# Paired projection in a hybrid GLA / Gated DeltaNet layer: x operands in two sets, fill slots and copies in another order

## The chip, the cores and the metric

One core of one Trainium2 chip, everything in float32. The metric is the device time of one execution in microseconds (us), the median of several runs. Engines are named as in the profile: PE (TensorE), PEld (its weight load), DVE (VectorE), ACT (ScalarE), POOL (GpSimd), SP (SyncE, which here only issues DMAs).

## The reference

One layer: RMSNorm, one input projection of 3608 columns, two head groups (GLA and Gated DeltaNet), an output projection with a residual, RMSNorm, and a gated MLP with a short convolution, for a prompt of 2048 tokens and eight sample sequences of four.

```python
hn = rmsnorm(x, norm1_g[l])
proj = hn @ w_in[l]                       # 1024 -> 3608
q_a, k_a, v_a, gate_a, low_a, qkv_b, z_b, beta_b, dec_b = jnp.split(proj, IN_IDX, axis=-1)
...
log_a = log_sigmoid(low_a @ gla_w_a2 + gla_b_a) / GLA_TAU
o_a, h_a = gla_chunked(q, k, v, log_a, st_gla[l])
o_a = rmsnorm(o_a, gla_norm_g) * silu(gate_a)
qkv, conv_new = causal_dwconv(qkv_b, st_conv[l], gdn_conv_w[l])   # width 4
qd, kd, vd = jnp.split(silu(qkv), ...)                            # q, k l2-normed
o_b, h_b = gdn_chunked(qd, kd, vd, g, beta, st_gdn[l])            # triangular solve in it
o_b = rmsnorm(o_b, gdn_norm_g) * silu(z_b)
x = x + concat(o_a, o_b) @ w_out[l]
x = x + (silu(a_f) * b_f) @ w_down[l]     # a_f, b_f: convolved up-projection of rmsnorm(x)
```

## The kernel before

The program has two stages. `mixers()` does all but the MLP, to 1765 us of the profiled execution; `mlp()` does the rest and is the same in both kernels. The prompt is cut into 16 tiles of 128 tokens (t = 0 to 15), and the sample is one more tile.

**One tile.** In each tile PE transposes the tile's `proj` (L1036 to L1059), multiplies for the decay sums (L1065 to L1077), and computes the GLA scores over seven levels (L1099 to L1104), which DVE copies with `turn_levels` (L1828). The short convolution is 48 DVE operations in four taps (`conv_tap`, L1846 and L1848) with a tanh on ACT (L1557) and the silu's end on DVE (L1959). The silu of both gates is two DVE operations (L1938). PE then transposes q, k and v (L1114, L1126, L1120), computes the GLA output (L1135, L1137), and inverts a triangular matrix in seven doubling levels a = 0 to 6. In each level POOL makes `ltm` (`ex<-dtt,level`, L842), PE multiplies (L1207, L1202), and DVE copies between. The state update and the outputs end the tile (L1281 to L1315); `gate_out` (DVE L2068) scales the outputs, and PE turns them (`turn_mixed`, L1196) for the next tile's output projection (L1002). `turn_y` (PE L1027) transposes the previous tile's normed sum.

**The input projection in the gaps.** Tiles 0 to 13 also compute the projection of the next pair of tiles by a Strassen-like scheme: 14 products per tile, each in two parts of two matmuls of 128x451. `fill(a, b)` in the PE program issues what stands in the slots a to b-1. `PRODUCT_SLOTS` gives the slot of each of the 28 parts, `OUT_SLOTS` that of each of 8 parts of the output projection. Three things feed the products:

- *Weight sums.* Ten chunks per tile, loaded by SP (`ring_chunk`, L526 from `sums_d`, L523 from the weights) into four places. A chunk's load waits until the products have used its place. The sums are made by DVE at the start (`first_sums`, `second_sums`, L1730) and stored by SP (L509).
- *x operands.* DVE scales two 128x1024 column blocks (`scaled_columns`, L1717) at the end of an even tile; POOL makes seven 128x512 operands from them in eight operations (L861 to L871) between an odd tile and the next.
- *Results.* ACT copies (`keep`, L1444) or DVE adds (`make_c11`, `make_c12`, `make_c22`, L1751) each product into one of eight `stage` buffers, SP stores them (L541), and `load_proj` (L553 to L560) reads the next tile's `proj`. `load_proj` waits for the gates' silu, the last reader of the old `proj`. The ring chunks n+4 and on (n = 10t) stand behind it in SP's order; the first product to read chunk n+4 is q = 6, parts 12 and 13.

The row scales of the columns take a way through memory: `store_scale` (L499) and `load_scales` (L504), both on SP.

**What sets the order.** Each engine's program is written out by hand in Python, with semaphores between them; no scheduler moves anything. A wait holds all that stands behind it on its engine. The two tables:

```python
OUT_SLOTS = {0: 0, 1: 1, 2: 2, 3: 3, 4: 4, 6: 5, 8: 6, 10: 7}
PRODUCT_SLOTS = {slot: p for p, slot in enumerate([5, 7, 9, 11, 12, 14, 15, 16, 17, 18, 20, 21, 22, 24] + list(range(25, 39)))}
```

## Time and profile before

| | |
|---|---|
| median of 3 runs | 3429.21 us (3424.32 to 3431.96) |
| profiled execution, its own time | 3427.54 us |
| its span, first to last instruction | 3425.8 us |
| mean granted TensorE clock, as a share of full speed | 0.957 |
| busy share of the span | PE 93%, DVE 62%, ACT 24%, POOL 19% |
| first projection and weight sums | 0 to 135.6 us |
| tiles 0 to 13, with the paired projection | 135.6 to 1532.0 us |
| tiles 14, 15 and the sample | 1532.0 to 1765.3 us |
| MLP | 1765.3 to 3425.8 us |

A tile is some 100 us: tile 4 begins (first L1077) at 523.71, tile 5 at 620.91 and tile 6 at 721.25 us. PE carries most of the work, so the time is what PE does, at the clock it is granted, and what it waits for. PEclk of 1.00 is 2.4 GHz and 0.50 is 1.2 GHz, the two levels that the profile shows. A row of a timeline may stand for several instructions ("x8"), whose first start and whole length it gives.

### The profile page before, as it was taken

Reading aid. Unit: us, or ns where it says so; the run is one execution under the profiler, and the core shown is the slowest. Engines: PE = TensorE matmul, PEld = TensorE weight load, DVE = VectorE, ACT = ScalarE, POOL = GpSimd, SP = SyncE. Lnnn points to the kernel's source line nnn. Section 1 sums busy time; section 2 is a strip of 40 time slices with the busy share of each in tenths; the row PEclk is TensorE's granted clock in tenths of the full one; section 3 lists DMA queues with packets and bytes.
Section 4 is the critical chain, followed back from the end, with each engine's and each line's share of the span. In section 5 each row is a group of like instructions: output and inputs, shape, how many; then the busy total and the mean of one; then the engine's idle time right before and its main releaser. Section 6 shows DMA issues by size and latency. Waiting matters only on the chain. (4 is left out here: it accounts for less than half of the span.)

```text
span 3425.8 us, 56382 instructions
## 1 busy us (share of the span) xinstructions
PE 3186.7 (93%) x22129; PEld 2094.5 (61%) x22129; DVE 2132.8 (62%) x4778; ACT 825.7 (24%) x1743; POOL 640.9 (19%) x985
## 2 busy tenths in 40 slices
PE   9699999999899998977679999999998999999999
PEld 4355555555555555544457777777767677767765
DVE  2666656666665666547555666656685665666668
ACT  1222222323132232212332121121222212212223
POOL 1212111120212112011223111112125121121110
PEclk9899999999999999988689999999999999999999
DMA  8655656556465656653561111111124111111112
GB/s 301 253 172 171 220 182 202 183 204 202 157 212 175 200 183 195 195 183 97 164 191 34 53 37 49 37 38 49 50 82 149 50 37 37 38 49 50 37 37 74
DMA packets 278999, 430.77 MB, mean 126 GB/s; under 512 B 20604, under 2 KB 203812, under 8 KB 277587
## 3 DMA queue, kind: packets, MB, share of 16 engines
q1 hardware_dynamic: 278739, 427.20, 38.8%
q8 instruction: 176, 2.88, 0.3%
q14 instruction: 84, 0.69, 0.1%
HBM read 361.44 MB, written 65.70 MB: 125 GB/s over the span
## 5 line engine op out<-in xcount | busy, mean ns | idle before, releaser
L970 PE MATMUL mixer_bank<-arena 128*128 128x451 f32 x1568 | 677.3, 562 | 0.4 <-issue 0.4
L2496 PE MATMUL mlp_bank<-arena,ws 128*128 128x256 f32 (+1 forms) x2816 | 648.3, 383 | 9.6 <-ACT raw L2686 9.6
L2496 PEld LDWEIGHTS mlp_bank<-arena,ws 128*128 128x128 f32 x2816 | 536.0, 190 | 92.8 <-ACT raw L2686 10.4
L2570 PE MATMUL mlp_bank<-arena 128*128 128x512 f32 x1120 | 493.9, 592 | 0.0
L970 PEld LDWEIGHTS mixer_bank<-arena 128*128 128x128 f32 x1568 | 281.6, 194 | 210.4 <-issue 204.3
L2971 DVE TENSOR_TENSOR acc<-acc,mlp_bank 128x512 f32<-128x512 f32 x560 | 370.3, 685 | 55.5 <-PE mlp_bank L2570 54.7
L2570 PEld LDWEIGHTS mlp_bank<-arena 128*128 128x128 f32 x1120 | 213.1, 190 | 234.5 <-issue 205.8
L842 POOL TENSOR_TENSOR ex<-dtt,level 128x512 f32<-128x512 f32 (+1 forms) x114 | 143.9, 1262 | 984.6 <-DVE dtt L1992 674.6
L2938 DVE SCALAR_TENSOR_TENSOR mcv<-raw,cf,mcv 128x512 f32<-128x512 f32 (+2 forms) x352 | 264.5, 767 | 59.4 <-ACT mcv L2659 50.6
L1002 PE MATMUL mixer_bank<-wo,th 128*128 128x512 f32 x512 | 266.3, 651 | 18.0 <-DMA wo<-in_w_out_dram 17.1
L2496 PE MATMUL mlp_bank<-arena 128*128 128x256 f32 (+1 forms) x1056 | 249.1, 386 | 5.3 <-PEq L3084 4.4
L2496 PE MATMUL mlp_bank<-arena,wu 128*128 128x256 f32 (+1 forms) x1056 | 246.0, 383 | 0.9 <-ACT raw L2688 0.9
L2496 PEld LDWEIGHTS mlp_bank<-arena 128*128 128x128 f32 x1056 | 201.1, 191 | 57.0 <-issue 26.4
L2496 PEld LDWEIGHTS mlp_bank<-arena,wu 128*128 128x128 f32 x1056 | 200.5, 190 | 49.2 <-issue 19.1
L2882 DVE TENSOR_TENSOR raw<-raw,mlp_bank 128x256 f32<-128x256 f32 (+1 forms) x88 | 37.5, 426 | 276.7 <-PE mlp_bank L2496 276.7
L1444 ACT COPY arena<-mixer_bank 128x451 f32<-128x451 f32 x112 | 59.7, 533 | 592.4 <-PE mixer_bank L970 592.3
L1002 PEld LDWEIGHTS mixer_bank<-wo,th 128*128 128x128 f32 x512 | 100.6, 208 | 142.8 <-issue 96.5
L2876 DVE TENSOR_TENSOR raw<-raw,mlp_bank 128x256 f32<-128x256 f32 (+1 forms) x88 | 37.5, 426 | 191.3 <-ACT raw L2688 191.3
L1848 DVE SCALAR_TENSOR_TENSOR cv<-cx,cw,cv 128x128 f32<-128x128 f32 x576 | 154.7, 344 | 0.0
L2659 ACT ACTIVATE mcv<-raw,cf 128x512 f32<-128x512 f32 (+2 forms) x176 | 126.8, 722 | 107.5 <-DVE raw L2882 85.6
L2642 ACT COPY raw<-mlp_bank 128x256 f32<-128x256 f32 (+1 forms) x88 | 33.1, 377 | 493.2 <-PE mlp_bank L2496 493.2
L2801 POOL COPY raws<-raw 128x32 f32<-128x32 f32 x44 | 7.8, 212 | 557.1 <-DVE raw L2882 557.1
(392 smaller groups left out, 4027.5 us busy)
## 6 DMA issues: line engine op xcount, KB each, us to landing
arena<-sums_d SPq DMA_DIRECT2D x112, 902.0 KB, 6.8
wo<-in_w_out_dram SPq DMA_DIRECT2D x260, 256.0 KB, 3.0
arena<-in_w_in_dram SPq DMA_DIRECT2D x44, 902.0 KB, 5.1
arena<-in_w_up_dram SPq DMA_DIRECT2D x44, 512.0 KB, 4.9
wu<-in_w_up_dram SPq DMA_DIRECT2D x44, 512.0 KB, 4.9
arena<-in_w_down_dram SPq DMA_DIRECT2D x40, 512.0 KB, 4.2
proj_d<-arena SPq DMA_DIRECT2D x84, 225.5 KB, 5.6
sums_d<-arena SPq DMA_DIRECT2D x16, 902.0 KB, 4.7
```

The costliest lines, as they stand in the source:

```text
L842: gp.tensor_tensor(ltm[0:N, :, 0:N], lt[0:N, :, 0:N], level[0:N, l, 0:N].unsqueeze(1).to_broadcast([N, H, N]), ALU.mult)\
L970: x = pe.matmul(out[:, 0:GW], xops[:, left, k, :], right[:, k, :], start=first and k == 0, stop=k == HK_IN - 1, skip_group_check=not first)
L1002: pe.matmul(bank[e if t == TILES else 3 + e][0:N, :], mixt[k // H][:, k % H, 0:N], wo[i % 4][:, :], start=(k == 0), stop=(k == KT - 1)).th ...
L1444: act.copy(stage[4 * (q // 7) + block], bank[source][:, 0:GW]).then_inc(s_kept, 1)
L1848: x = dve.scalar_tensor_tensor(out=dst, in0=src, scalar=cw[:, c, tap:tap + 1], in1=dst, op0=ALU.mult, op1=ALU.add)
L2496: x = pe.matmul(out[:, 0:N], left[:, k, :], xb[:, slot, k, g * N:(g + 1) * N], start=first and k == 0, stop=k == HK - 1, skip_group_check= ...
L2570: pe.matmul(bank[4 + o % 4][:, :], left, right, start=True, stop=True).then_inc(s_down_done, 1)
L2659: act.activation(cv[e][:, 0:n], raw[p][e][:, c0:c0 + n], ACT.Identity, scale=cf[p][:, e, 0:1])\
L2876: dve.tensor_tensor(v, v, q_bank[:, 0:N], ALU.add).then_inc(s_q1_added, 1)
L2882: dve.tensor_tensor(v, v, q_bank[:, 0:N], ALU.add).then_inc(s_q2_added, 1)
L2938: x = dve.scalar_tensor_tensor(out=dst, in0=src, scalar=w, in1=dst, op0=ALU.mult, op1=ALU.add)
L2971: dve.tensor_tensor(v, v, bank[4 + o % 4][:, :], ALU.add).then_inc(s_y_added, 1)
```

## The change

1. The order of the first projection, of its weight loads and of the sums: all four `first_sums` come ahead of all four `second_sums`, the stores follow that order, and the 16 `wo` chunks are loaded behind them.
2. The x operands lie in two sets (`x_set`, `sum_set`), used in turn. POOL makes a pair's operands in six operations, two of them 128x1024, in steps behind levels a = 2 to 6 of the odd tile before. DVE's two column scalings stand in levels a = 4 and 5 of the even tile.
3. `stage` has four buffers and not eight; two `keep`s wait for stores.
4. The two tables of slots; `turn_y(0)` and `turn_y(1)` go from level a = 1 to a = 2 and 3, the DVE work behind them likewise.
5. On ACT, `qsq` and `ked` stand ahead of the sum's norm and the next x tile's norm.
6. The gates' silu stands behind the GLA levels and `make_c22(t, 0)`. The convolution's end is split: tanh of q and k, then of v, and three silus with a semaphore step each; `turn_levels(3, 6)` goes ahead of `make_c11(t, 0)`.
7. The scaling of `hgdn` stands ahead of a reduce at the tile's end; `store_scale`, `load_scales` and `store_hs` move in SP's order.

```diff
-FIRST = [(g, tile) for g in (4, 0, 5, 1, 6, 7) for tile in range(2)] + [(2, 1), (3, 1), (2, 0), (3, 0)]
+FIRST = [(g, tile) for g in (4, 5, 6, 7, 0, 1) for tile in range(2)] + [(2, 1), (3, 1), (2, 0), (3, 0)]
-OUT_SLOTS = {0: 0, 1: 1, 2: 2, 3: 3, 4: 4, 6: 5, 8: 6, 10: 7}
-PRODUCT_SLOTS = {slot: p for p, slot in enumerate([5, 7, 9, 11, 12, 14, 15, 16, 17, 18, 20, 21, 22, 24] + list(range(25, 39)))}
+OUT_SLOTS = {0: 0, 1: 1, 2: 2, 3: 3, 4: 4, 6: 5, 9: 6, 11: 7}
+PRODUCT_SLOTS = {slot: p for p, slot in enumerate([5, 7, 10, 12] + list(range(14, 26)) + [27] + list(range(29, 40)))}
...
+                if t < TILES - 4:
+                    store_scale(t + 4)
                 ring_chunk(n + 8)
                 if even:
                     store_block(t, 0, C12)
                 store_block(t, 0, C21)
+                if t < TILES - 4 and not even:
+                    load_scales(t + 3)
...
+                    if prepares and a >= 2:
+                        x_operands((t + 1) // 2, (a - 2,))
+            def x_operands(p, steps):
+                source = (xc, hnt) if p == 0 else x_of(p)
+                if 0 in steps:
+                    gp.wait_ge(s_rsb_loaded, 16 * (p + 1))
+                    gp.wait_ge(s_xg_made, p + 1)
...
+                for e in range(2):
+                    if e in steps:
+                        gp.tensor_tensor(x_of(p)[e][:, :, :], source[e][:, :, :],
+                                         rsb[:, e, :].unsqueeze(1).to_broadcast([C, KT, C]), ALU.mult)\
+                            .then_inc(s_xops_made, 1)
+                if 2 in steps:
+                    gp.tensor_tensor(s1, a21, a22, ALU.add).then_inc(s_xops_made, 1)
+                if 3 in steps:
+                    gp.tensor_tensor(s2, s1, a11, ALU.subtract).then_inc(s_xops_made, 1)
+                    gp.tensor_tensor(a21, a11, a21, ALU.subtract).then_inc(s_xops_made, 1)
+                if 4 in steps:
+                    gp.tensor_tensor(s4, a12, s2, ALU.subtract).then_inc(s_xops_made, 1)
...
+                act.wait_ge(s_q_turned, n)
+                act.activation(qsq[0:N, :, :], heads(3)[0:N, :, :], ACT.Square).then_inc(s_q_squared, 1)
+                act.wait_ge(s_kl_turned, n)
+                act.copy(ked[0:N, :], bank[6][0:N, 256:512]).then_inc(s_ked_out, 1)
...
                 if out and not sample:
                     y_square(t, C)
-                    act.wait_ge(s_y_normed, 3 * t - 2)
+                    y_log(t, C)
+                    y_root(t, C)
                 front(0)
+                front(1)
+                front(2)
...
                 if hosts:
                     make_c22(t, 0)
+                for g, c0 in enumerate((O_GA, O_Z)):
+                    dve.wait_ge(s_gates_tanh, 3 * t + g + 1)
+                    dve.scalar_tensor_tensor(out=gate[...], in0=gate[...], scalar=1.0,
+                                             in1=proj[0:N, c0:c0 + H * DV], op0=ALU.add, op1=ALU.mult)\
+                        .then_inc(s_gates_silu, 1)
...
+            first_sums(2, 4)
+            first_sums(3, 6)
             dve.wait_ge(s_xc_loaded, 32)
...
-            second_sums(1, 6)
-            first_sums(2, 8)
-            first_sums(3, 10)
+            second_sums(0, 8)
+            second_sums(1, 10)
```

**PE, the inverse of tile 4, levels 0 to 3** (L970 is half a product, L1207 a level's multiply, L1027 `turn_y`). Before:

```order
L970 MATMUL mixer_bank<-arena 128x451 x2
L1257 MATMUL mixer_bank<-ident,qe 128x128 x4
L1207 MATMUL mixer_bank<-qe,ex 32x16 x16
L1027 MATMUL mixer_bank<-ident,xr 128x128 x4
L1207 MATMUL mixer_bank<-ex,qe 32x16 x16
L1207 MATMUL mixer_bank<-qe,ex 32x16 x16
L1027 MATMUL mixer_bank<-ident,xr 128x128 x4
L970 MATMUL mixer_bank<-arena 128x451 x4
L1207 MATMUL mixer_bank<-qe,ex 32x16 x16
L970 MATMUL mixer_bank<-arena 128x451 x2
L1207 MATMUL mixer_bank<-qe 32x16 x32
```

After, where L995, L1233 and L1052 are the same three:

```order
L995 MATMUL mixer_bank<-arena 128x451 x2
L1281 MATMUL mixer_bank<-ident,qe 128x128 x4
L1233 MATMUL mixer_bank<-qe,ex 32x16 x16
L995 MATMUL mixer_bank<-arena 128x451 x2
L1233 MATMUL mixer_bank<-ex,qe 32x16 x16
L1233 MATMUL mixer_bank<-qe,ex 32x16 x16
L995 MATMUL mixer_bank<-arena 128x451 x4
L1233 MATMUL mixer_bank<-qe,ex 32x16 x16
L1052 MATMUL mixer_bank<-ident,xr 128x128 x4
L1233 MATMUL mixer_bank<-qe 32x16 x32
L995 MATMUL mixer_bank<-arena 128x451 x2
L1233 MATMUL mixer_bank<-qe,ex 32x16 x16
```

The two transposes of `turn_y` stood with their copies between the levels a = 1; product parts stand there now, and `turn_y` one and two levels later.

**ACT in tile 4, from the convolution's tanh to the copy of ked** (L1448 squares the previous sum, L1420 the next x tile, L1572 is `qsq`). Before:

```order
L1444 COPY arena<-mixer_bank 128x451
L1557 ACTIVATE th<-cv 128x1536
L1444 COPY arena<-mixer_bank 128x451
L1562 ACTIVATE dtt<-dtt 128x512
L1563 ACT_TABLE_LOAD
L1448 ACTIVATE cx,y_ss<-yo 128x8x128
L1420 ACTIVATE cx,x_ss<-xt 128x8x128
L1572 ACTIVATE th<-mixer_bank 128x512
L1453 ACTIVATE y_ln<-y_ss,eps 128x1
L1578 COPY ked<-mixer_bank 128x256
L1458 ACTIVATE y_rs<-y_ln 128x1
L1463 ACTIVATE xr<-yo,y_rs 128x1024
```

After:

```order
L1467 COPY arena<-mixer_bank 128x451
L1580 ACTIVATE th<-cv 128x1024
L1582 ACTIVATE th<-cv 128x512
L1467 COPY arena<-mixer_bank 128x451
L1587 ACTIVATE dtt<-dtt 128x512
L1588 ACT_TABLE_LOAD
L1590 ACTIVATE th<-mixer_bank 128x512
L1594 COPY ked<-mixer_bank 128x256
L1471 ACTIVATE cx,y_ss<-yo 128x8x128
L1476 ACTIVATE y_ln<-y_ss,eps 128x1
L1481 ACTIVATE y_rs<-y_ln 128x1
L1443 ACTIVATE cx,x_ss<-xt 128x8x128
```

`ked` went ahead of both squares of 128x1024, and the tanh is in two pieces.

**SP in tile 5, from the load of proj to the load of scales** (sums_d is a ring chunk, scale_d the row scale). Before:

```order
L556 DMA proj<-proj_d 128x2x902
L526 DMA arena<-sums_d 128x1804 x2
L575 DMA resid<-yo 128x1024
L526 DMA arena<-sums_d 128x1804
L541 DMA proj_d<-arena 128x451
L523 DMA arena<-in_w_in_dram 128x4x451
L526 DMA arena<-sums_d 128x1804
L541 DMA proj_d<-arena 128x451
L591 DMA xr<-in_x_prompt_dram 128x1024
L582 DMA hn_t<-yo 128x8x128
L526 DMA arena<-sums_d 128x1804
L499 DMA scale_d<-x_rs 128x1
L504 DMA xt<-scale_d 128x256
```

After:

```order
L575 DMA proj<-proj_d 128x2x902
L546 DMA arena<-sums_d 128x1804 x2
L594 DMA resid<-yo 128x1024
L546 DMA arena<-sums_d 128x1804
L560 DMA proj_d<-arena 128x451
L543 DMA arena<-in_w_in_dram 128x4x451
L519 DMA scale_d<-x_rs 128x1
L546 DMA arena<-sums_d 128x1804
L560 DMA proj_d<-arena 128x451
L524 DMA xt<-scale_d 128x256
```

Behind `proj`, the scale's store stood after six ring chunks (L526 and L523) and stands after four now; its load stood right behind it, and has one more chunk and a block's store ahead of it now.

## Rows read from the trace of the kernel before

**Rows 1.** Windows: window, length, busy PE PEld DVE ACT POOL, PEclk, DMA share, GB/s.

```profile
...
0.00:135.60 135.60, 103.63 (x293) 53.10 (x293) 46.39 (x53) 22.91 (x50) 28.61 (x54) 0.92 0.79 286
...
231.60:1532.00 1300.40, 1189.11 (x12338) 706.63 (x12337) 820.45 (x2352) 347.06 (x712) 218.87 (x243) 0.95 0.59 191
1532.00:1765.30 233.30, 166.88 (x2289) 104.78 (x2287) 148.11 (x472) 72.16 (x187) 37.47 (x51) 0.77 0.44 130
1765.30:3425.80 1660.50, 1640.80 (x6286) 1179.29 (x6286) 1055.05 (x1714) 358.11 (x741) 343.90 (x622) 0.99 0.19 57
```

**Rows 2.** Waits of PE, 231.6 to 1532 us: us in all, times, longest.

```profile
...
PE mixer_bank L1135 <- ACT ked L1578: 26.4, 13, 2.1
PE mixer_bank L1196 <- DVE th L2068: 24.7, 13, 1.9
PE mixer_bank L1002 <- DMA wo<-in_w_out_dram: 14.6, 2, 14.0
PE mixer_bank L1065 <- DVE gg L1866: 12.5, 6, 3.8
PE mixer_bank L1027 <- DVE hgla L2042: 10.5, 13, 0.8
PE mixer_bank L1207 <- DVE ex L2087: 10.1, 13, 0.8
```

**Rows 3.** Waits of PE, 1532 to 1765 us, same columns.

```profile
...
PE mixer_bank L1114 <- DVE cv L1959: 8.7, 2, 4.7
```

**Rows 4.** Timelines of DVE, ACT and PE ahead of tile 0.

```profile
...
118.71 4.11 DVE L1730 TENSOR_TENSOR arena<-arena 128x1804 f32<-128x1804 f32 x2 [3.60 <-DMA sums_d<-arena]
...
132.76 0.63 ACT L1490 ACTIVATE qe<-mixer_bank,ba 128x128 f32<-128x128 f32 x2 [20.89 <-DMA proj_d<-qe]
...
134.46 0.59 PE L1065 MATMUL mixer_bank<-gg,incl 128*128 128x4 f32 x2 [22.74 <-DVE gg L1866]
```

**Rows 5.** Timeline of PE, tile 4.

```profile
...
563.12 1.68 PE L970 MATMUL mixer_bank<-arena 128*128 128x451 f32 x4
...
578.37 0.45 PE L1207 MATMUL mixer_bank<-qe,ex 128*32 128x16 f32 x32
```

**Rows 6.** Timeline of ACT, tile 4.

```profile
...
551.93 1.06 ACT L1448 ACTIVATE cx<-yo 128x1024 f32<-128x1024 f32 x1
...
553.12 1.06 ACT L1420 ACTIVATE cx<-xt 128x1024 f32<-128x1024 f32 x1
...
554.84 0.36 ACT L1578 COPY ked<-mixer_bank 128x256 f32<-128x256 f32 x1
```

**Rows 7.** Timeline of DVE, tiles 4 and 5.

```profile
...
513.23 6.17 DVE L1846 TENSOR_SCALAR cv<-cx,cw 128x128 f32<-128x128 f32 x12 [2.02 <-ACT cx L1482]
...
533.96 1.28 DVE L1938 SCALAR_TENSOR_TENSOR gate<-gate,proj 128x512 f32<-128x512 f32 x2
...
552.79 0.62 DVE L1751 TENSOR_TENSOR arena<-arena,mixer_bank 128x451 f32<-128x451 f32 x1
...
612.84 2.44 DVE L1846 TENSOR_SCALAR cv<-cx,cw 128x128 f32<-128x128 f32 x12 [1.62 <-ACT cx L1482]
```

**Rows 8.** Timeline of POOL, tile 4.

```profile
...
574.54 1.27 POOL L842 TENSOR_TENSOR ex<-dtt,level 128x512 f32<-128x512 f32 x1 [7.01 <-PE mixer_bank L1207]
```

**Rows 9.** DMA issues, 530 to 560 us (tile 4): times, KB each, us to landing.

```profile
...
arena<-sums_d SPq DMA_DIRECT2D x3, 902.0 KB, 8.9
proj<-proj_d SPq DMA_DIRECT2D x1, 1804.0 KB, 10.1
```

**Rows 10.** DMA issues, 620 to 722 us (tile 5), same columns.

```profile
...
proj<-proj_d SPq DMA_DIRECT2D x1, 902.0 KB, 7.2
...
xt<-scale_d SPq DMA_DIRECT2D x1, 128.0 KB, 5.5
scale_d<-x_rs SPq DMA_DIRECT2D x1, 0.5 KB, 8.9
```

**Rows 11.** DMA issues, 145 to 160 us (tile 0), same columns.

```profile
...
proj<-proj_d SPq DMA_DIRECT2D x1, 1804.0 KB, 7.3
```

More of the change, by code:

```diff
@@ L116, in mixers @@
         wx, wy = ([v.rearrange("p (k n) -> p k n", k=HK_IN) for v in f] for f in (x_flat, y_flat))
-        xops = arena[:, at_y:at_y + 7 * HK_IN * C].rearrange("p (b k i) -> p b k i", b=7, k=HK_IN)
-        stage = [arena[:, at_y + 2 * HW + b * GW:at_y + 2 * HW + (b + 1) * GW] for b in range(8)]
+        x_sets_at, stage_at, sums_at = at_y, at_y + 2 * HW, at_y + 2 * HW + 4 * GW
+        stage = [arena[:, stage_at + b * GW:stage_at + (b + 1) * GW] for b in range(4)]
         def weight(k, g):
@@ L540, in store_block @@
                 tile = t - t % 2 + 2 + (block in (C21, C22))
-                sp.dma_start(p_d[tile, :, c0:c0 + GW], stage[b]).then_inc(s_stage_stored, 16)
+                sp.dma_start(p_d[tile, :, c0:c0 + GW], stage[block]).then_inc(s_stage_stored, 16)
             def load_proj(t):
@@ L620, in _ @@
             store_sum(15, P_T4, 3, y_flat[3])
+            for i in range(4):
+                wo_chunk(0, i)
             sp.wait_ge(s_one_out, GROUPS)
@@ L819, in mixer @@
                 levels = SAMPLE_LEVELS if sample else range(NL)
+                prepares = not sample and t % 2 == 1 and t < HOSTS - 1
                 ready(gp, t)
@@ L873, in _ @@
+            x_operands(0, range(5))
             mixer(0, 1, False, False)
@@ L969, in product @@
                 for k in range(2 * half, 2 * half + 2):
-                    x = pe.matmul(out[:, 0:GW], xops[:, left, k, :], right[:, k, :], start=first and k == 0,
+                    x = pe.matmul(out[:, 0:GW], x_operand(t // 2, left)[:, k, :], right[:, k, :], start=first and k == 0,
                                   stop=k == HK_IN - 1, skip_group_check=not first)
@@ L1228, in mixer @@
                         x.then_inc(s_xi_turned, 1)
-                    if a == 1 and not sample:
-                        turn_y(0)
-                        fill(23, 24)
-                    else:
-                        fill(22 + 2 * a, 23 + 2 * a)
+                    if a in (2, 3) and not sample:
+                        turn_y(a - 2)
+                    fill(*((23, 24) if a == 1 and not sample else (22 + 2 * a, 23 + 2 * a)))
                     if sample:
@@ L1556, in mixer @@
                 tq = th_s if sample else th
[L1557 removed]
+                act.activation(tq[:, 0:8, 0:N], cv[:, 0:8, 0:N], ACT.Tanh, scale=0.5).then_inc(s_conv_tanh, 1)
+                act.wait_ge(s_tap, 5 * n)
+                act.activation(tq[:, 8:12, 0:N], cv[:, 8:12, 0:N], ACT.Tanh, scale=0.5).then_inc(s_conv_tanh, 1)
                 if hosts:
@@ L1567, in mixer @@
                     y_square(t, C)
-                    act.wait_ge(s_y_normed, 3 * t - 2)
+                    y_log(t, C)
+                    y_root(t, C)
                 front(0)
-                act.wait_ge(s_q_turned, n)
-                act.activation(qsq[0:N, :, :], heads(3)[0:N, :, :], ACT.Square).then_inc(s_q_squared, 1)
+                front(1)
+                front(2)
                 if out and not sample:
-                    y_log(t, C)
-                act.wait_ge(s_kl_turned, n)
-                if not sample:
-                    act.wait_ge(s_sg_done, t)
-                act.copy(ked[0:N, :], bank[6][0:N, 256:512]).then_inc(s_ked_out, 1)
-                if out and not sample:
-                    y_root(t, C)
                     y_scaled(t, C)
@@ L1849, in conv_tap @@
                                                          in1=dst, op0=ALU.mult, op1=ALU.add)
+                        if tap == 3 and c == 7:
+                            x.then_inc(s_tap, 1)
                     x.then_inc(s_tap, 1)
@@ L2101, in mixer @@
                         make_c12(t, 0)
-                    if a == 1 and out and not sample:
-                        keep_y_half(t, C, 0)
                     if a == NL - 1:
@@ L2136, in mixer @@
                         gate_out(0)
+                        if out and not sample:
+                            keep_y_half(t, C, 1)
+                    if a in (4, 5) and not sample and t % 2 == 0 and t < TILES - 4:
+                        scale_pair(t, a - 4)
                 if hosts:
@@ L2175, in mixer @@
                     add_gla(0, 2)
+                if not sample:
+                    dve.wait_ge(s_od_done, n)
+                    dve.tensor_tensor(hgdn[:, :, :], hgdn[:, :, :],
+                                      egrow[:, :, C - 1:C].to_broadcast([C, H, DV]), ALU.mult)\
+                        .then_inc(s_sd_scaled, 1)
                 dve.wait_ge(s_o_squared, 2 * n)
```

197 lines of the change are left out of this document (92 added, 105 removed).

## Prediction

> **What bounds the kernel now.** I read the windows by stage first, then PE's waits in the tile stage, then the timelines around the waits, then the DMA landings. By the windows [rows 1] PE is busy 1189.1 of 1300.4 us in tiles 1 to 13, 166.9 of 233.3 us in tiles 14 to 16, 103.6 of 135.6 us in the first projection, and 1640.8 of 1660.5 us in the MLP, which the change does not touch. So the time is PE's work plus PE's idle time, and the part that can go is the 111.3 us idle in the tile stage, some of the 66.4 us behind it, and the 32 us ahead. The waits [rows 2] say what the 111.3 us are. The copy of `ked` costs 26.4 us (13 tiles, 2.1 at most), `th` from `gate_out` 24.7 (13, 1.9), `gg` 12.5 (6, 3.8), `hgla` 10.5 (13, 0.8), `ex` in the levels 10.1 (13, 0.8); 14.6 is a load of `wo` (14.0 of it in one piece), which no edit moves. Without that load 96.7 us are left, 7.4 per tile. Ahead of tile 0 PE waits 22.74 us in one piece [rows 4]. The clock is the second reader of a wait: PEclk is 0.95 in tiles 1 to 13 against 0.99 in the MLP [rows 1]. With the two levels 2.4 and 1.2 GHz as 1.0 and 0.5, a mean of 0.95 is 10% of the stretch, 130 us, at the low one.
>
> **The change part by part, in tiles 1 to 13.**
>
> *ked on ACT.* Before, two squares of 1.06 us stand ahead of it from 551.93 on and `ked` comes at 554.84 [rows 6]; PE waits 2.0 us for it in the mean. Without the two squares `ked` is some 2.1 us earlier or more (two rows of 1.06), and the silu of q and k, which need only the first tanh, comes earlier too. The 26.4 us go to nothing; I count them all.
>
> *gg.* It is waited for in six of 13 tiles, that is once per pair, when POOL makes its eight operands: in tile 4 the 12 operations of tap 0 take 6.17 us, in tile 5, without POOL's work beside them, 2.44 [rows 7]. That work leaves this place, so 12.5 us go. It comes to lie beside the levels of the odd tiles, where DVE mostly reads PSUM; I count no slowing there, and at most 1 us per odd tile (a quarter of the 3.7 above) in the range.
>
> *th.* One product part goes from the first half to slot 39, ahead of `turn_mixed`: a part is 1.68 us [rows 5], and the scaling of `hgdn` ahead of the reduce takes a little off DVE's chain. Together they are worth about the 1.9 us wait, so the 24.7 us go.
>
> *turn_y.* Waits for `hgla` and `ex` are 1.6 us per tile now (10.5 + 10.1 over 13), and the rest of the 96.7 us, a part of it here too, is 12.5, 1.0 per tile. In their place stand product parts of 1.68 us, with a single part where the copy of a level takes longer. I estimate what remains: 0.3 at the first GLA levels, 0.3 and 0.6 in levels 1 and 4, 0.45 at the second `turn_y`, 0.4 of issue. That is 2.05 us per tile, from no row but the size of those waits (0.8 at most each); between 1.0 and 3.5.
>
> *New wait 1: the ring chunk behind load_proj.* SP's `load_proj` waits for the gates' silu. It is done at 535.2 in tile 4 (533.96 + 1.28) and stands now behind `make_c22(t, 0)`, which ends at 553.4 (552.79 + 0.62) [rows 7]. What is queued behind it on SP are all ring chunks from n+4, and part 12 reads chunk n+4. In the trace before that slot's place is PE's 563.12 [rows 5], 9.7 us behind the end of c22. Take off the 2.1 us wait for `ked` that goes and 1.28 for the silu that comes between, and put back some 1.0 for DVE's chain, which is no longer waiting for one long tanh: the chunk must land 7.3 us after SP issues `load_proj`. In even tiles `proj` is 1804 KB and goes first. Alone it landed in 7.3 us [rows 11]; half as much behind it at the same rate is 3.65, so the chunk lands between 7.3 and 10.95 after, I take the middle and an issue of 0.3: 9.4, a wait of 2.0 us. With other traffic beside it both landed in 10.1 and 8.9 [rows 9]; with `ring_chunk` issued 2.2 us behind, as a bound, that is 12.3 and a wait of 5. In odd tiles `proj` is 902 KB, 7.2 us to landing [rows 10]; the chunk at 8.3, a wait of 1.0, at most 2.6. Sum: 6 times 2.0 and 7 times 1.0, 19 us, in a range of 0 to 48.
>
> *New wait 2: the scales, in odd tiles 1 to 11.* POOL makes its first operand behind level 2 and only then level 3's `ltm`. I count from the place of slot 22 (563.12 in tile 4). The scale's store stands behind the fourth chunk, whose place is free when slot 21 is done, 2 us ahead (one multiply of the state and one of `ked` lie between). It lands 8.9 later and the load 5.5 behind that [rows 10], at +12.4. The operand is twice the size of the row of 1.27 us [rows 8], 2.5, and `ltm` is that row: +16.2. PE wants level 3 at 578.37, +15.3 [rows 5]; with the two waits of 0.8 gone and one `turn_y` fewer ahead, +13.2, and 1.0 later for new wait 1. What is left is 2.0; with small delays of SP between its queue's rows (some 0.4) I take 2.4, six times: 14 us. It is nothing if the scales land 3 us earlier, and double if the store leaves 2.4 us later.
>
> Here a rule speaks for a better outcome. The Trainium skill, "DMA: Bandwidth & Descriptors", section "Latency and other measured facts", gives the fixed cost of a DMA as about 2 us; the row of a store of 0.5 KB has 8.9 us. By the page the scales would be there 6 us earlier and new wait 2 would be nothing, 14 us less. The row decides for the sum; the store's 128 separate values and the queue ahead of it are in it and not in the rule.
>
> *Sum for the stage.* Idle after: 13 times 2.05 is 26.7, plus 19, plus 14, 60 (from 96.7): **-37 us**.
>
> *Clock.* Low stretches follow waits. Idle and low time should fall together; of the 130 us low, idle and slow work are about equal parts, and slow work loses half of its time, so some 30 us are lost in all. With 35 to 40% fewer of them: **-12 us** (between 0 and -20).
>
> **Ahead of tile 0.** PE waits from 111.7 to 134.46 for the chain behind `proj_d<-qe`, a store for which ACT stood 20.89 us; DVE's last pair of sums began at 118.71 after a wait of 3.6 for the stores of `sums_d` [rows 4]. SP issues the store of the second tile's `proj` only behind all 16 stores of sums. In the new order a place is rewritten once all first sums are out, eight stores later and not two to four, so stores stream instead of waiting in turn with DVE, and the end comes some 15 to 20 us earlier; then it is PE's own end (its last matmuls at about 111.7) plus a landing, by 4.5 us. So the 22.74 us shrink to 4.5: **-18 us**; bounds 0 (the DMA queues are the limit: their share is 0.79 [rows 1]) and -22.7.
>
> **Tiles 14 and 15.** No products there, and DVE's chain is waited for: the convolution's silu 8.7 us [rows 3]. Split in q, k and v, with the gates' silu behind, it is some 3 to 4 us per tile shorter: **-7 us** (0 to -12). The MLP: nothing.
>
> **Sum.** -37 - 12 - 18 - 7 = -74. The profiled execution took 3427.5 us itself, 1.7 under the median of the runs shown. 3427.5 - 74 is **3354 us**, 2.1% faster.
>
> **The rivals.** A difference under 0.2% (7 us) can't be told from none.
> *A, the new waits hide.* Chunk and scales land in time: 33 us less, and 8 less at the low clock: 3313. For it: the DMA share is 0.59, so there are gaps. Against it: every landing of these loads in [rows 9, 10] is over 7 us. 0.20.
> *B, they cost double.* Wait 1 at its bounds (+29) and wait 2 doubled (+14): 3397. For it: rows 9 were taken under the traffic that such a place has. 0.17.
> *C, slower.* One mechanism: chunk n+4 behind `load_proj`. The sum is used up when it lands 5.7 us later (74 over 13 tiles), 15 us after the issue and not 9.4. At 16 us the time is 3354 + 13 x 6.6, about 3440. The rows allow 12.3, so this needs traffic that no row shows. 0.04.
> *D, the start does not move,* because DMA and not the order bounds it: 3372. 0.07.
> *E, the scales come at the skill's price*, the mechanism of new wait 2 without its delay: 3340. Only the one row is against it. 0.07.
> *F, nothing comes of it,* the freed time goes to other waits of PE, such as levels 2 and 3 on DVE: 3427. 0.03.
> My forecast, with a range of its own from 3335 to 3375, has 0.42.
>
> **How the numbers follow.** From 3308 (A, with 5 us for its own spread) to 3400 (B, the like) leaves out C and F, and a third each of A and B, on their outer sides: 0.19. Faster by over 0.2%: all but C, F and a remnant of B, 0.93. Within: 0.03. Slower: 0.04.
>
> **What would show it.** Right: no wait of PE for `ked`, `gg` or `th` over 0.3 us; a wait at the first part 12 for a DMA of `sums_d`, 2 us in even tiles; in odd tiles a wait of 2 to 3 us at level 3 for POOL's `ltm`, with POOL waiting on `xt<-scale_d`; one wait of 3 to 6 us ahead of tile 0; PEclk of the tile stage at 0.97. Wrong: a tile's period over 97 us, a wait at part 12 over 4 us, or the stores of sums still ending at 125 us.

## The result

The changed kernel takes 3402.46 us (median of 8 runs, 3394.48 to 3412.83) against 3429.72 us (median of 8, 3420.78 to 3437.41) of the kernel before on the same chips: a ratio of 0.9925, 95% interval 0.9905 to 0.9944. It is faster by 0.75%, where 2.1% and 3354 us were forecast, and it lies just outside the forecast's range of 3308 to 3400. The direction was right and the size was wrong.

The profiled execution took 3395.82 us itself, with a span of 3394.1 and a mean clock of 0.962. Its windows, for the stages of [rows 1], with a stage for tile 0 (window, length, busy us of PE, PEld, DVE, ACT and POOL, PEclk, DMA share, GB/s):

```profile
0.00:117.10 117.10, 104.44 (x294) 53.24 (x294) 44.96 (x53) 24.19 (x52) 21.87 (x52) 1.00 1.00 344
117.10:213.80 96.70, 86.77 (x926) 51.52 (x927) 63.28 (x189) 25.16 (x54) 12.03 (x15) 0.90 0.56 170
213.80:1503.50 1289.70, 1147.29 (x12338) 684.13 (x12337) 788.70 (x2352) 348.67 (x725) 213.52 (x231) 0.96 0.59 193
1503.50:1735.00 231.50, 171.46 (x2292) 107.42 (x2291) 150.00 (x474) 72.84 (x190) 39.06 (x54) 0.76 0.44 131
1735.00:3394.10 1659.10, 1639.45 (x6284) 1178.10 (x6283) 1055.11 (x1713) 358.09 (x741) 343.07 (x620) 0.99 0.19 57
```

The span of the profiled execution is 31.7 us shorter than that of the kernel before. The start gives 18.5 of it (135.6 to 117.1 us), tiles 1 to 13 give 10.7 (1300.4 to 1289.7), tiles 14 to 16 1.8, the MLP 1.4, and tile 0 costs 0.7. In tiles 1 to 13 two large movements cancel. PE ran the same 12338 matmuls in 1147.3 us and not in 1189.1, so its work takes 42 us less; its idle time rose from 111.3 to 142.4 us, by 31. Both had been forecast to fall, the work by 12 and the idle time by 37.

PE's waits in that stage (us in all, times, longest), to be set beside [rows 2]:

```profile
PE mixer_bank L1233 <- POOL ex L864: 59.9, 6, 10.4
PE mixer_bank L1027 <- DMA wo<-in_w_out_dram: 30.2, 16, 18.8
PE mixer_bank L995 <- DMA arena<-sums_d: 21.8, 13, 3.3
PE mixer_bank L1233 <- issue: 13.6, 8, 5.9
PE mixer_bank L1233 <- DVE qe L2117: 7.3, 11, 0.8
PE mixer_bank L1233 <- DVE ex L2117: 6.1, 7, 1.8
```

Gone are the waits for `ked` (26.4), `th` (24.7), `gg` (12.5) and `hgla` (10.5). In their place is one of 59.9 us in six pieces of up to 10.4, for `ltm` on POOL, and one of 21.8 us for the ring chunk (2.1 to 3.3 us in each even tile, 0.2 to 1.5 in each odd one); the waits for `wo` went from 14.6 to 30.2, and those without a cause that the profile shows ("issue") to 13.6 at this one line, 5.9 at the longest (3.4 in the kernel before).

The places of these waits in tile 5. SP's timeline (start, length, line, out<-in):

```profile
641.08 0.53 SPq L575 DMA_DIRECT2D proj<-proj_d  x1
641.66 2.43 SPq L546 DMA_DIRECT2D arena<-sums_d  x2
...
646.24 0.38 SPq L543 DMA_DIRECT2D arena<-in_w_in_dram  x1
646.67 0.53 SPq L519 DMA_DIRECT2D scale_d<-x_rs  x1
...
654.70 0.32 SPq L560 DMA_DIRECT2D proj_d<-arena  x1
663.19 0.32 SPq L524 DMA_DIRECT2D xt<-scale_d  x1
```

The first row is `load_proj`. Within 5.6 us of it SP issues four ring chunks (two in the row x2, one at 644.61, one at 646.24), a residual store, a block store and then the scale's store, which leaves at 646.67, 5.6 us behind `load_proj`. The load of the scales goes out at 663.19, when the store is complete: 16.5 us. POOL and PE:

```profile
667.74 2.34 POOL L884 TENSOR_TENSOR xc<-xc,xt 128x1024 f32<-128x1024 f32 x1 [13.64 <-DMA xt<-scale_d]
670.03 1.26 POOL L864 TENSOR_TENSOR ex<-dtt,level 128x512 f32<-128x512 f32 x1
```

```profile
649.82 1.75 PE L995 MATMUL mixer_bank<-arena 128*128 128x451 f32 x4 [1.54 <-DMA arena<-sums_d]
...
671.35 0.63 PE L1233 MATMUL mixer_bank<-qe,ex 128*32 128x16 f32 x32 [9.97 <-POOL ex L864]
```

POOL's first operand starts at 667.74, its next `ltm` at 670.03, and PE has waited 9.97 us when level 3 starts. The wait for the chunk, at 649.82, is 1.54 us.

The start, beside [rows 4]: one wait of 2.94 us where there were 22.74. SP's last store of the sums is out at 93.7 us, and was at 123.2.

```profile
115.89 0.39 PE L1090 MATMUL mixer_bank<-gg,incl 128*128 128x4 f32 x2 [2.94 <-DVE gg L1893]
```

Tiles 14 and 15, beside [rows 3]:

```profile
PE mixer_bank L1222 <- DVE th L2098: 6.6, 2, 3.8
...
PE mixer_bank L1161 <- DVE at L1858: 4.7, 2, 3.4
...
PE mixer_bank L1139 <- DVE cv L1978: 3.3, 2, 2.1
```

The wait for the convolution's silu fell from 8.7 to 3.3 us, but 4.7 us for `at` of the GLA scores took `ked`'s place there. In the whole stage (the windows above and [rows 1]) PE's idle time fell from 66.4 to 60.0 us, and its busy time rose from 166.9 to 171.5, with PEclk at 0.76 and not 0.77.

### The profile page after: what moved, and what is told of

Same layout as the page of the kernel before. It is cut to its first block and busy times, and to the rows that moved or that the text cites. A ratio compares the mean times of both kernels' runs of the same rounds, so it can differ in the third digit from the quotient of the medians.

```text
span 3394.1 us, 56405 instructions
## 1 busy us (share of the span) xinstructions
PE 3149.4 (93%) x22129; PEld 2074.4 (61%) x22129; DVE 2102.0 (62%) x4778; ACT 829.0 (24%) x1760; POOL 629.5 (19%) x971
## 5 line engine op out<-in xcount | busy, mean ns | idle before, releaser
L2528 PEld LDWEIGHTS mlp_bank<-arena,ws 128*128 128x128 f32 x2816 | 536.0, 190 | 92.8 <-ACT raw L2718 10.4
L995 PE MATMUL mixer_bank<-arena 128*128 128x451 f32 x1184 | 512.8, 565 | 14.9 <-DMA arena<-sums_d 14.7
L995 PEld LDWEIGHTS mixer_bank<-arena 128*128 128x128 f32 x1184 | 214.5, 195 | 177.8 <-issue 173.8
L1027 PE MATMUL mixer_bank<-wo,th 128*128 128x512 f32 x512 | 250.1, 619 | 33.5 <-DMA wo<-in_w_out_dram 33.2
L1027 PEld LDWEIGHTS mixer_bank<-wo,th 128*128 128x128 f32 x512 | 93.2, 193 | 141.9 <-issue 73.2
L1233 PE MATMUL mixer_bank<-qe,ex 128*32 128x16 f32 (+1 forms) x3328 | 60.1, 196 | 77.3 <-POOL ex L864 59.9
```

The lines of the kernel that those rows point to most:

```text
L995: x = pe.matmul(out[:, 0:GW], x_operand(t // 2, left)[:, k, :], right[:, k, :], start=first and k == 0, stop=k == HK_IN - 1, skip_group_ch ...
L1027: pe.matmul(bank[e if t == TILES else 3 + e][0:N, :], mixt[k // H][:, k % H, 0:N], wo[i % 4][:, :], start=(k == 0), stop=(k == KT - 1)).th ...
L1233: x = pe.matmul(packed(out[k, b // 2:(b + width) // 2], l), left[:, k], blocks(right[:, k], l, r), start=True, stop=True)
L2528: x = pe.matmul(out[:, 0:N], left[:, k, :], xb[:, slot, k, g * N:(g + 1) * N], start=first and k == 0, stop=k == HK - 1, skip_group_check= ...
```

## The experiments

Times are medians against the kernel before, measured on the same chip; ratios have their 95% interval. "The changed kernel" is the one above, 3402.46 us and 0.9925. The runs were made on several chips, so a small difference between two of them is better read from the ratios: 0.001 is 3.4 us. The waits shown are PE's in tiles 1 to 13, up to 1480 us (1500 in experiment 1).

**1. The scale's store behind one chunk.** Theory Q: the store's way takes so long because SP's issues stand ahead of it.

```diff
                 ring_chunk(n + 4)
+                if t < TILES - 4:
+                    store_scale(t + 4)
...
                 ring_chunk(n + 7)
-                if t < TILES - 4:
-                    store_scale(t + 4)
```

> Only the store of the row scale moves: in SP's order it stands behind one ring chunk instead of four. Theory Q (queue): the store takes 16.5 us in tile 5 of the changed kernel because SP issues the load of proj, four chunks and two stores within 6 us once the gates' silu is done, and the store's bytes stand behind them; early, it lands in 7 to 9 us, PE's wait for ltm of level 3 (59.9 us in six tiles, 10.4 at most) falls to 10 to 20 us in all, and the time to about 3365 us. Rival P (POOL's own work between the levels, 2.3 us for the first multiply and 1.3 for ltm behind it): the wait stays over 40 us and the time over 3390. Rival S (the load's place in SP's order behind the store of C21): the load is issued at the same place, the wait falls only to about 50.

Measured: 3393.15 us, 0.9899 (0.9879 to 0.9919).

```profile
PE mixer_bank L1233 <- POOL ex L864: 34.4, 7, 7.6
...
PE mixer_bank L995 <- DMA arena<-sums_d: 30.0, 13, 6.6
```

The wait at level 3 fell from 59.9 to 34.4 us, less far than Q said and further than P and S allow; the time is what P gave. From the store's issue to the load's it took 11.6 to 14.6 us in five of the six tiles, and 20.7 once. That is no longer the time of the store. The load leaves as soon as SP comes to it, right behind the block's store:

```profile
645.18 0.54 SPq L560 DMA_DIRECT2D proj_d<-arena  x1
645.77 0.74 SPq L524 DMA_DIRECT2D xt<-scale_d  x1
```

SP waits for the scale's store 1.0 us in all six tiles together, and 54.0 in the changed kernel. So the mechanism of rival S is there: SP's order sets when the load leaves. But the load now takes 9.2 to 11.7 us to land in five of the tiles, where it took 3.5 to 4.5. Counted from the issue of `load_proj`, the wait at level 3 ends 28.0 to 30.2 us later, and 29.4 to 30.3 in the changed kernel. So the scales came only some 1 us sooner. The rest of the fall is PE coming later: the chunk's wait rose from 21.8 to 30.0 us (6.4 of it in tile 9), and one of 4.6 for a copy on ACT is new.

**2. POOL's steps behind levels 4 to 6.**

```diff
-                    if prepares and a >= 2:
-                        x_operands((t + 1) // 2, (a - 2,))
+                    if prepares and a >= 4:
+                        x_operands((t + 1) // 2, ((0,), (1, 2), (3, 4))[a - 4])
```

> POOL's six x operations stand behind levels 4, 5 and 6 in place of levels 2 to 6; the scale's way stays as it is. Theory Q: the scales land before POOL wants them, at most 1 us of wait per odd tile is left, 55 us of idle go, and the time is 3340 to 3355 us. Rival P: the same POOL work in fewer levels makes the waits longer there, 20 us or more in all at levels 5 and 6.

Measured: 3365.65 us, 0.9819 (0.9802 to 0.9835). No wait for POOL is left among PE's largest; of what the steps' work could have cost, the wait for DVE's `ex` is 8.6 us now (6.1 in the changed kernel):

```profile
PE mixer_bank L995 <- DMA arena<-sums_d: 21.7, 13, 3.2
...
PE mixer_bank L1233 <- DVE ex L2117: 8.6, 9, 2.4
```

The scale's way is still 16.0 to 16.8 us in each of the six tiles. So the stall came through POOL's order: `ltm`, which PE needs, stood behind an operand that waits for a DMA. P falls. Of the 60 us of waits 37 came back as time, less than the 47 to 62 that were expected, and no run says why. Of the first tiles the odd ones fell by 7 to 9 us each (1, 3 and 5 from 100.6, 101.2 and 101.5 to 93.6, 92.6 and 94.1), and the even ones stayed (2, 4 and 6 at 97.1, 99.4 and 96.4, and at 97.2, 98.1 and 97.9).

**3. The gates' silu back in its place.**

```diff
+                for g, c0 in enumerate((O_GA, O_Z)):
+                    ...
+                        .then_inc(s_gates_silu, 1)
                 if not sample:
                     turn_levels(0, ROUND)
...
                     make_c22(t, 0)
-                for g, c0 in enumerate((O_GA, O_Z)):
-                    ...
-                        .then_inc(s_gates_silu, 1)
```

> The gates' silu goes back ahead of the first turn_levels, all else stays. Theory Q: load_proj is issued some 10 us earlier, the chunk wait (24.3 us in 14) goes to nothing, the issues are spread again, the scale's store lands in about 9 us and the wait at level 3 falls to under 20 us; DVE's chain is 1.3 us longer ahead of the convolution, worth up to 1 us per tile: time about 3350. If the level 3 wait is POOL's or the scale's own way, the time falls only by the chunk wait, to about 3385.

Measured: 3351.57 us, 0.9782 (0.9765 to 0.98). This one edit undone is worth 51 us, and the time is what was expected of Q (about 3350). That it is near the forecast's 3354 us is chance: the forecast had the silu late.

```profile
PE mixer_bank L1233 <- POOL ex L864: 21.6, 6, 5.2
```

The chunk's wait is gone from the list and the one at level 3 is 21.6 us (under 20 were expected). SP in tile 5:

```profile
602.51 0.53 SPq L575 DMA_DIRECT2D proj<-proj_d  x1
607.14 4.23 SPq L546 DMA_DIRECT2D arena<-sums_d  x2
...
622.65 0.50 SPq L519 DMA_DIRECT2D scale_d<-x_rs  x1
...
632.92 0.32 SPq L524 DMA_DIRECT2D xt<-scale_d  x1
```

`load_proj` leaves 20 us ahead of the scale's store and not 5.6, the four chunks leave in four places, and the scale's way takes 10.3 us (9.4 to 10.3 in six tiles) and not 16.5.

**4. POOL's steps behind the last level.**

```diff
-                    if prepares and a >= 2:
-                        x_operands((t + 1) // 2, (a - 2,))
...
                 mixer(t, t + 1, False, True)
+                if t % 2 and t < HOSTS - 1:
+                    x_operands((t + 1) // 2, range(5))
```

> POOL makes all x operands behind the odd tile's last level as before the change, with the two sets kept. Theory Q: the wait for ltm goes (60 us), the wait for gg comes back (12.5 us in six tiles before the change) because POOL's work lies beside tap 0 again: about 3355 us. Rival P expects the same here; so this run says what steps in the levels are worth at best.

Measured: 3362.15 us, 0.9798 (0.9781 to 0.9814). The same as with steps behind levels 4 to 6, within the intervals. PE did not wait for `gg` again (the expectation had 12.5 us), because POOL's work does not come to lie beside tap 0 again. In tile 5 its last operand is made at 676.65 us, and DVE begins tap 0 at 687.36, in 2.44 us as without POOL:

```profile
675.38 1.27 POOL L896 TENSOR_TENSOR arena<-xc,arena 128x512 f32<-128x512 f32 x1
...
687.36 2.44 DVE L1871 TENSOR_SCALAR cv<-cx,cw 128x128 f32<-128x128 f32 x12 [2.79 <-ACT cx L1505]
```

So the steps in the levels were not needed to free `gg`. That the two sets and the earlier load of the scales let POOL begin sooner is read from the program; no run took them apart. The chunk's wait stayed, at 23.5 us.

**5. ACT's order undone.**

```diff
+                if out and not sample:
+                    y_square(t, C)
+                    act.wait_ge(s_y_normed, 3 * t - 2)
+                front(0)
                 act.wait_ge(s_q_turned, n)
                 act.activation(qsq[0:N, :, :], heads(3)[0:N, :, :], ACT.Square).then_inc(s_q_squared, 1)
...
                 act.copy(ked[0:N, :], bank[6][0:N, 256:512]).then_inc(s_ked_out, 1)
...
-                    y_square(t, C)
-                    y_log(t, C)
...
-                front(0)
```

> Of the changed kernel only the order on ACT is undone: the two squares of 128x1024 stand ahead of the square of q and of the copy of ked again. Theory: the wait at the first GLA output comes back, 1.5 to 2 us in each of 14 tiles, and with it a stretch at the low clock behind each, which costs more work time than the forecast's 12 us in all; so the time rises by 30 to 50 us against the changed kernel, to 3430 to 3450. Rival: the edit is worth its wait at most and the long wait at level 3 takes most of it up: 3402 to 3415 us.

Measured: 3404.2 us, 0.9928 (0.9912 to 0.9945), the time of the changed kernel. The theory fell here, the rival held.

```profile
PE mixer_bank L995 <- DMA arena<-sums_d: 12.6, 9, 2.5
PE mixer_bank L1161 <- ACT ked L1602: 12.4, 12, 1.0
```

The wait for `ked` is back, at 12.4 us, and the chunk's is down from 21.8 to 12.6, level 3's from 59.9 to 51.9. PE waits for `ked` two product parts ahead of the part that waits for the chunk: what it arrives earlier it waits longer. So the early copy of `ked` was worth nothing in this kernel, within the some 9 us that the intervals leave.

**6. The new start alone, on the kernel before.** Only the first part of the change: the order of the groups, the loads, the sums and their stores.

```diff
-FIRST = [(g, tile) for g in (4, 0, 5, 1, 6, 7) for tile in range(2)] + [(2, 1), (3, 1), (2, 0), (3, 0)]
+FIRST = [(g, tile) for g in (4, 5, 6, 7, 0, 1) for tile in range(2)] + [(2, 1), (3, 1), (2, 0), (3, 0)]
...
             first_sums(1, 2)
-            second_sums(0, 4)
+            first_sums(2, 4)
+            first_sums(3, 6)
...
-            first_sums(2, 8)
-            first_sums(3, 10)
+            second_sums(0, 8)
+            second_sums(1, 10)
```

> The kernel before with the first part of the change alone (the order of the first projection, of its loads, of the sums and their stores). Tile 0 begins 17 to 19 us earlier and nothing else moves: 3410 to 3413 us. Rival: the later tiles, whose loads meet the start's stores no more, move as well, by more than 3 us either way.

Measured: 3411.44 us against 3430.71, 0.9945 (0.9923 to 0.9966), 19 us.

```profile
115.79 0.39 PE L1066 MATMUL mixer_bank<-gg,incl 128*128 128x4 f32 x2 [2.94 <-DVE gg L1867]
```

The 2.94 us wait is that of the changed kernel to the digit. The forecast's -18 for the start is shown, alone and in the whole. The rival is not settled: in the profiled execution, itself 7.6 us over the median, tiles 1 to 13 took 1306.4 us and not 1300.4.

**7. The scale's store on ACT's queue.**

```diff
                 front(2)
+                if not sample and t < TILES - 4:
+                    act.wait_ge(s_x_normed, 3 * (t + 4) + 3)
+                    act.dma_start(rs_d[(t + 4) * C:(t + 5) * C, :], x_rs[:, t % 4:t % 4 + 1], allow_slow_non_contiguous=True)\
+                        .then_inc(s_rs_stored, 16)
...
-                if t < TILES - 4:
-                    store_scale(t + 4)
```

> The changed kernel with the store of the row scale issued by ACT right behind the value (642.4 us in tile 5), and not by SP. Theory Q, a queue of SP's own: without SP's 5 MB ahead of it the store lands within 4 us, the load goes out when SP comes to it (654.7) and lands about 5 us later, the wait at level 3 falls from 60 to about 15 us and the time to about 3365. Rival R, the engines that carry all queues are full: the store still takes 10 us and more, and the wait stays at 30 to 60 us.

Measured: 3422.82 us, 0.9973 (0.9963 to 0.9983), slower than the changed kernel by 20 us, or by 16 if one goes by the ratios.

```profile
PE mixer_bank L993 <- DMA arena<-sums_d: 76.5, 13, 9.0
PE mixer_bank L1231 <- POOL ex L862: 24.7, 6, 4.6
```

DMA issues of 640 to 652 us, tile 5 (times, KB each, us to landing):

```profile
arena<-sums_d SPq DMA_DIRECT2D x3, 902.0 KB, 13.1
proj<-proj_d SPq DMA_DIRECT2D x1, 902.0 KB, 5.4
...
scale_d<-x_rs ACTq DMA_DIRECT2D x1, 0.5 KB, 10.6
```

On a queue of its own the store of half a KB still takes 10.6 us, and 10.6 to 13.6 in the six odd tiles. Q's 4 us fall, and for the store R holds. How much of the 16.5 us belongs to SP's queue this run does not say, since the place changed with the queue: the store leaves 1.3 us behind `load_proj` and not 5.6, with less ahead of it.

That the two queues share the work of the DMA engines is seen in the chunk. Here the first chunk behind `load_proj` lands in 12.6 us in tile 5. In run 1, where the store stands right behind the same chunk, but on SP's queue, it landed in 8.3 (this run first, then run 1):

```profile
arena<-sums_d SPq DMA_DIRECT2D x1, 902.0 KB, 12.6
```

```profile
arena<-sums_d SPq DMA_DIRECT2D x1, 902.0 KB, 8.3
```

The Trainium skill, "DMA: Bandwidth & Descriptors", section "Issuing engines are not separate DMA queues", says the same: transfers end up on the same 16 DMA engines whoever issues them. The chunk's 12.6 us agree with it. That the store makes the chunk this much later that section does not say. But this run shows that it is the store: in tiles 1 to 11, which store a scale, PE waits 5.5 to 9.1 us for the chunk, and in tiles 12 and 13, which store none, 2.5 and 1.8, as in the changed kernel (2.4 and 1.5). Why it costs so much no run here took apart.

The wait at level 3, 24.7 us, lies between the two theories' figures and tests neither. Behind a chunk whose place PE frees late, SP issues the load of the scales only at 669.64 us, 9.4 behind the store's landing, and PE too comes later.

**8. Silu back and late steps together.** Edits 2 and 3.

> The gates' silu back ahead of the first turn_levels and POOL's x operations behind levels 4 to 6. Each alone gave 3351.6 and 3365.7 us. Both new waits go: the 21.6 us that were left at level 3 with the silu back go too, with some low clock: 3325 to 3335 us. Rival: POOL's work in the levels is then the next wait, and the time stays at 3345 or more.

Measured: 3323.14 us, 0.9698 (0.968 to 0.9716). Both new waits are gone, and the time is 2 us under what was expected; the most that PE waits for at its levels now:

```profile
PE mixer_bank L1233 <- issue: 19.4, 12, 3.9
```

**9. Chunk n+4 ahead of load_proj.**

```diff
+                ring_chunk(n + 4)
                 load_proj(t + 1)
-                n = CHUNKS * t
-                even = t % 2 == 0
-                ring_chunk(n + 4)
```

> The changed kernel with ring chunk n+4 ahead of load_proj in SP's order, nothing else. The chunk is issued as soon as its place is free and not when the gates' silu is done. The wait at part 12 for sums_d (24.3 us in 14) goes to under 3 us. Theory of a shared burst: level 3's wait for ltm, which is set by the scale's way, takes up what is freed in the six odd tiles, and only the even tiles gain: 3385 to 3392 us. Rival: the burst is a chunk smaller and the scale lands earlier too: 3365 to 3378.

Measured: 3375.85 us, 0.9842 (0.9822 to 0.9862). The chunk's wait is gone. The rival held for the rest: level 3's wait fell too, by 13 us,

```profile
PE mixer_bank L1233 <- POOL ex L864: 46.8, 6, 8.5
```

and the scale's way took 13.6 to 14.9 us and not 16.1 to 16.8. One chunk fewer ahead of the store made the way 2.4 us shorter in the mean of the six tiles. An estimate from bytes agrees: 902 KB at 334 GB/s, the rate of the changed kernel's burst in tile 5 (shown in the next section), are 2.7 us.

**10. ACT's order undone where no chunk is waited for.** Edit 5 on kernel 8.

> The order on ACT is undone as in the fifth run, but on the kernel with the silu back and the late steps, which has no chunk wait behind it. There the undoing cost nothing (3404.2 against 3402.5), and the chunk wait fell from 24.3 to 12.6 us. Theory: ked's early copy was worth nothing because the chunk wait stands between it and the next work; without the chunk wait it is worth its 12 to 26 us and some clock: 3340 to 3355 us. Rival: it is worth nothing anywhere: 3320 to 3328.

Measured: 3345.62 us, 0.9754 (0.9736 to 0.9772) against 0.9698 of kernel 8: 19 us by the ratios, give or take 9.

```profile
PE mixer_bank L1161 <- ACT ked L1602: 15.2, 13, 2.7
```

With the chunk's wait out of the way the same edit is worth its wait, 15.2 us, and perhaps more.

**11. Chunk n+4 first and late steps, silu left late.** Edits 2 and 9.

> The changed kernel with ring chunk n+4 ahead of load_proj and POOL's steps behind levels 4 to 6; the gates' silu stays late. If the two new waits are all that is wrong with the late silu, this reaches the time of the kernel with the silu back and the late steps (3323 us) or less: 3320 to 3330. Rival: the burst behind the silu costs in further ways (late stores of blocks, the wo chunks, issue): 3340 to 3350.

Measured: 3326.78 us, 0.9686 (0.9656 to 0.9716), as fast as kernel 8 within the intervals. So once neither the chunk nor `ltm` hangs on it, no cost of the late silu can be told from none: the two waits are nearly all that was wrong with it. (Kernel 8 lacks edit 9, so the two differ in more than the silu; kernel 12, with all four edits, is 0.003 faster, also within the intervals.)

**12. All four edits.** 2, 3, 9 and 1 together.

> The silu back and the late steps (3323.1 us) with, on top, chunk n+4 ahead of load_proj and the scale's store behind one chunk. Neither the chunk nor the scale is waited for there any more, so both further edits are off the path: 3315 to 3330 us. Rival: the earlier chunk and store take DMA time from the load of proj or of wo and cost 5 us or more: over 3330.

Measured: 3318.57 us against 3437.88, 0.9655 (0.9637 to 0.9673), the fastest, 2.7% under the changed kernel. Whether it is faster than kernels 8 and 11 is not settled: the intervals of 11 and 12 overlap, and those of 8 and 12 miss each other by 0.0007 on different chips. Its tiles 1 to 13:

```profile
206.90:1419.70 1212.80, 1136.78 (x12338) 677.35 (x12337) 787.07 (x2351) 348.68 (x725) 214.37 (x231) 0.98 0.67 205
```

PE's idle time is 76.0 us there and PEclk 0.98, where the changed kernel had 142.4 and 0.96.

## Why the prediction was wrong, step by step

**Ahead of tile 0: right.** -18 forecast, -18.5 in the trace, 19 us alone (run 6). The mechanism is there too: the stores of the sums end 29.5 us earlier, and PE waits for its own last projection.

**ked, gg, th, turn_y: the waits went as forecast.** None of the first three is left in tiles 1 to 13 (63.6 us of them before), and what is left at the levels, 2.3 us per tile, is near the 2.05 of the forecast, though half of it is "issue", for which the forecast had 0.4. For *ked*, "The 26.4 us go to nothing; I count them all" was right as a reading. The forecast also saw that PE then comes to the chunk 2.1 us earlier. What it did not have is that this takes back the whole gain: run 5 shows that the early copy was worth nothing in this kernel, and run 10 that it is worth some 19 us in another. A wait ahead of another wait whose end is fixed is no saving.

**New wait 1, the chunk: right.** 19 us forecast, 21.8 measured in 13 tiles (24.3 with tile 0): 2.7 us per even tile for 2.0, and 0.8 per odd tile for 1.0. Its mechanism is shown by runs 3 and 9, which take it away.

**New wait 2, the scales: the step that failed.** The forecast had 14 us, the trace 59.9. The step reads "It lands 8.9 later and the load 5.5 behind that". The 8.9 was read where one chunk had left right ahead of the store (683.62 and 683.98 us) and the stream was spread otherwise. Here it comes 5.6 us behind `load_proj`, with four chunks, `proj` and two stores ahead of it, about 5 MB, and takes 16.5 us. In that stretch the DMA engines are full, 0.99 of the time at 334 GB/s:

```profile
641.10:659.10 18.00, 16.46 (x229) 11.10 (x231) 11.29 (x26) 4.83 (x13) 4.59 (x6) 1.00 0.99 334
```

At that rate 5 MB take 15 us; that is an estimate of the work ahead of the store. The count from slot 22 was right: PE would have waited some 2 us with 8.9. The 7.6 us more that the store took are the 7.6 us more that PE waited (9.97 against 2.4). Run 3 (a spread stream: 10.3 us, 21.6 of wait) and run 9 (one chunk fewer: 14 us, 46.8) give the steps between. Run 1, with the store early, only moved the delay from the store to the load. Run 7 says that another queue does not take the store out of the burst, and run 2 that the price comes about through POOL's order, where `ltm` stands behind the operand. The forecast had the burst in hand (it gave the late silu as the reason for the chunk's wait) and did not carry it to the next DMA in the same stream. Its rival B ("they cost double") was nearest, and too small for this wait: it was four times. That B's 3397 us lies near the 3402 measured is luck: its wait 1 did not double, and the clock gave back what B did not count.

**The rule that the forecast weighed**, the fixed cost of about 2 us in the Trainium skill, "DMA: Bandwidth & Descriptors", section "Latency and other measured facts", lay further off than the row: by it the wait would have been nothing. The store took 16.5 us here; a fixed cost says nothing of what is ahead. (8.9 less 2 is also 6.9 us and not 6, which changes nothing.)

**Clock: the mechanism right, the size wrong.** -12 us forecast, -42 measured as PE's busy time for the same 12338 matmuls. The step that failed is "idle and slow work are about equal parts". The granted clock and PE's busy times in the two traces, laid over each other, show it. In the kernel before, the clock is at 1.2 GHz for 133.1 us of tiles 1 to 13, and PE is busy in 119.7 of them: nearly all is slow work. In the changed kernel it is there for 109.2 us, and PE is busy in 51.3 and idle in 57.9. So 68 us less of work ran at 1.2 GHz, worth 34 us at half speed. This is an estimate, and it leaves 8 of the 42 us unexplained. One low stretch of each kernel, tile 4 before and tile 5 after (length, busy time of PE first, PEclk third from the end):

```profile
568.00:571.40 3.40, 3.26 (x70) 2.54 (x71) 3.09 (x7) 0.00 (x0) 0.00 (x0) 0.51 0.02 5
```

```profile
666.00:676.20 10.20, 4.85 (x103) 3.36 (x104) 1.18 (x3) 0.09 (x1) 8.46 (x7) 0.50 0.25 58
```

Before, the waits were short (0.8 to 2.1 us) and came at two or three places in a tile, and the clock was low for work behind them. The output projection behind `th` took 216.9 us in tiles 1 to 13 (L1002) and takes 199.6 now, the transposes of `proj` 30.9 (L1055) and now 20.8, and the two lines of the GLA output behind `ked` 23.3 and 23.0, and now 20.1 each. The mean clock hardly moved, 0.95 to 0.96, because over half of the low time now is the long waits of level 3 themselves. So the mean clock of a stage does not say how much work runs slowly. That the low stretches follow waits is seen in the rows of both kernels; a run that changes only the clock was not made.

**Tiles 14 and 15:** -7 forecast, -1.8. The wait at the convolution went from 8.7 to 3.3 us as forecast; 4.7 us for `at` came in behind it, but `ked`'s 4.5 went. PE's idle time in the stage fell by 6.4 us, close to the forecast; what took it back is PE's work, 4.6 us longer. The step that failed is that the sum took the work of this stage as unchanged. Whether the clock (PEclk 0.76 for 0.77) made it longer is not shown.

**Not forecast:** the waits for `wo`, 14.6 to 30.2 us, of which 18.8 (14.0 before) is one in tile 14's loads and the rest 0.3 to 1.3 at a tile's start, and "issue", which rose at the levels from 3.4 to 13.6 us. One of these lies amid 32 matmuls of one level in tile 4:

```profile
565.06 0.23 PE L1233 MATMUL mixer_bank<-qe,ex 128*32 128x16 f32 x5
571.16 0.61 PE L1233 MATMUL mixer_bank<-qe,ex 128*32 128x16 f32 x27 [5.88 <-issue]
```

The burst is over by then: the DMA share from 565.3 to 571.2 us is 0.12. These waits stayed in kernels without the burst too (19.4 us in kernel 8). What they are stays open.

The sum by its terms, forecast and trace: start -18 and -18.5; idle of tiles 1 to 13 -37 and +31; its work -12 and -42; tiles 14 to 16 -7 and -1.8; the rest 0 and -0.7. The miss of 42 us between the spans: idle time of tiles 1 to 13 was 68 us over the forecast (142.4 against 60 and 14.6 for `wo`), of which 46 is wait 2, 16 `wo`, 3 the chunk and 4 all the rest; tiles 14 to 16 add 5; and the clock takes 30 off again. Of the forecast's own signs of being wrong, one came: a tile's period is 99.2 us in the mean, and not under 97. The wait at part 12 stayed under 4 us (3.3 at most), and the stores of the sums ended at 93.7 us and not at 125.

## What to carry to other kernels

A DMA's duration belongs to its place: before a landing time is taken from a row, count what will be issued shortly ahead of it in the new order. When an edit delays a load, what stands behind it in the same queue leaves in one burst, and here a tiny transfer paid most, because its reader (POOL, with `ltm` behind) stood ahead of work that PE needed. Put work that waits for a DMA behind the work that others wait for; that one line was worth 37 us, and with the silu's place 79.
